# One encoder layer with retrieved experts: projections and attention moved between the expert pairs, three tiles at a time

## The chip, the cores and the metric

One core of a Trainium2 chip runs one launch of the kernel, all in float32. The metric is the device time of that launch in microseconds. Before the change it is 4207.86 us, the median of three runs (4206.48 to 4216.56).

## What is computed

One layer over 1024 prompt tokens and 8 x 16 sample tokens: nine tiles of 128 tokens (eight of the prompt, PT, and one of the samples, ST) by 1024 features.

```python
q_sb, k_sb, v_sb, q_sw, k_sw, v_sw, q_mem, gates = split_projection(rmsnorm(x, norm_mix), w_in, b_gate)
o_sb  = sb_attend(...)    # stick-breaking, 8 heads x 64, over all earlier tokens
o_sw  = sw_attend(...)    # window of 128, 8 heads
o_mem = mem_attend(...)   # 4 heads x 128 into 256 memory tokens
x = x + (sum_b gates_b * (o_b @ w_o_b)) @ w_out
xb = rmsnorm(x, norm_ffn)
# product-key retrieval: 8 heads, the best 16 of 128 x 128 experts each = 128 experts per token
s = einsum('thpd,hpkd->thpk', xb @ w_q, keys);  idx, g = softmax of the best 16 per head
a = gelu(einsum('thkd,td->thk', u_tab[idx], xb))
x = x + einsum('thk,thkd->td', g * a, v_tab[idx])
```

A token's row of expert tables is 2 x 1024 floats (u and v), 8 KB. So a gather of one expert slot for the 128 tokens of a tile is 1 MB, and there are 9 x 128 = 1152 of them, 1208 MB in all. Stick-breaking attention of prompt tile t reads the key blocks t, t-1, ... 0; tiles 0 to 7 make 36 steps of (query tile, key block), the samples two more.

## The kernel before

`build` (L1696) runs three parts, each a block of its own, with every engine's instructions written out by hand and ordered by semaphores.

- `project` (L83): normalises and transposes the nine tiles and two tiles of memory, and makes all of q, k, v. Weight blocks of 2 MB are the outer loop, the tiles the inner one; a unit is eight matmuls into one PSUM bank (L315, and L310 for q of the stick-breaking branch). 61 units.
- `attend` (L527): a software pipeline over steps of time `tau` from the tables of `Course` (L466). A stick-breaking step starts every two `tau` and goes from engine to engine: scores on PE (L815), |z|, exp, ln on ScalarE (L867 to L871), softplus on VectorE (L905), running sums on PE (L682, L685), exp on ScalarE (L829), the carried sum on VectorE (L894), values on PE (L744). Beside it run 27 window and memory units.
- `experts` (L1068): gates, output projections, queries, scores and ranking of a group of tiles (a `Front`, L975, again steps `tau`: the gates' matmuls L1340 and L1350, the output's L1365, the queries' L1388), and the expert pairs. The groups are (0, 1), (2, 3, 4), (5, 6, 7, 8).

The expert part is a sequence of 576 **ticks**, 64 for a tile, each with a **pair** of slots. GpSimd gathers a slot into a ring of RING = 10 buffers (L1311) when PE has released the buffer. VectorE takes the dot product of the u half with the token's row `xp`, which lies in PSUM (L1674, twice a tick). ScalarE makes the gelu (L1497), the weight (L1504, twice) and a diagonal matrix of it (L1510, twice). PE multiplies the v half by the diagonals and adds up in PSUM (L1416, eight matmuls a tick), and so releases the buffers. After its part of the pair each engine does `advance`: the steps `tau` of the next group's Front that `PACES` (L1027) gives this tick. On PE it stands behind the pair's sums. Every second tick VectorE also does a piece of the ranking (`top`, L1531; three pieces for each of a tile's eight heads) of the tiles that are not the first of their group.

```python
            advance(0)
            for m in range(NT):
                for q in range(NB):
                    if q == 0:
                        advance(1 + m * NB)
                    accumulate(m, q)
                    if q:
                        advance(1 + m * NB + q)
```

Of the kernel before, what the change touches and what calls it, by code (L numbers as in the profile page):

```python
# [20 lines left out]
TOK = NT * P  # L31
DB, DS = 8, 16
HD = 64
MH, MD, MT = 4, 128, 256
# [9 lines left out]
RING = 10  # L44
BATCH = 2
NB = SLOTS // BATCH
GROUPS = ((0, 1), (2, 3, 4), (5, 6, 7, 8))
PARTS = (2, 3, 4)
HALF = P // 2
# [29 lines left out]
WQ = 2 * PH * P  # L79
# [3 lines left out]
def project(nc, A, S, small_dram, hT_d):  # L83

    ident = S["const"][:, 0:P]
    hT, mhT, ps = S["hT"], S["mhT"], S["ps"]
    with ExitStack() as ctx:  # L87
        sb = lambda n, s, dt=F32: ctx.enter_context(nc.sbuf_tensor(n, s, dt))
        sem = lambda n: ctx.enter_context(nc.semaphore(n))
        w = S["shared"][:, 0:2 * KC * HB].rearrange("p (a k n) -> p a k n", a=2, k=KC)  # L90
        stage = S["shared"][:, 2 * KC * HB:2 * KC * HB + 4 * HB].rearrange("p (a n) -> p a n", a=4)
        gmix = sb("gmix", [P, 2, KC])
        gq = sb("gq_heads", [P, 2 * HD + 2 * MD])
        ss = sb("ss", [P, 3])
        nrm = sb("nrm", [P, 3, 8])
        XR = 4
        xt = [S["vsb"][:, 2 * i:2 * i + 2, :].rearrange("p a n -> p (a n)") for i in range(XR)]
        sqt = stage[:, 3, :]

        const_in = sem("const_in")  # L100
        gains_in = sem("gains_in")
        gmix_in = sem("gmix_in")
        x_in = [sem(f"x_in{i}") for i in range(XR)]
        w_in = [sem(f"w_in{i}") for i in range(2)]
        x_sq = sem("x_sq")
        x_ms = sem("x_ms")
        x_rt = sem("x_rt")
        x_rs = sem("x_rs")
        x_nat = sem("x_nat")
# [4 lines left out]
        squared = sem("squared")  # L114
        summed = sem("summed")
        mean = sem("mean")
        rooted = sem("rooted")
# [7 lines left out]
        v_out = sem("v_out")  # L125
        cache_out = sem("cache_out")
        spilled = sem("spilled")

        TILES = [A["x_prompt"][0, t * P:(t + 1) * P, :] for t in range(PT)]
        TILES += [A["x_sample"].rearrange("b s d -> (b s) d")]  # L130
        TILES += [A["mem_prompt"][0, t * P:(t + 1) * P, :] for t in range(2)]
        NX = len(TILES)

        w_v = A["w_in"][0].rearrange("(c p) n -> p c n", p=P)
        wm_v = A["w_mem_kv"][0].rearrange("(c p) n -> p c n", p=P)

        BLOCKS = [("ksb", w_v[:, :, 512:1024], 512, range(NT)), ("vsb", w_v[:, :, 1024:1536], 512, range(NT)),
                  ("kvsw", w_v[:, :, 2048:2304], 256, range(NT)), ("qsw", w_v[:, :, 1536:2048], 512, range(NT)),
                  ("qm", w_v[:, :, 2304:2816], 512, range(NT)), ("mk", wm_v[:, :, 0:512], 512, range(2)),
                  ("mv", wm_v[:, :, 512:1024], 512, range(2)), ("qsb", w_v[:, :, 0:512], 512, range(12))]  # L140
        units = [(c, kind, t) for c, (kind, _, _, tiles) in enumerate(BLOCKS) for t in tiles]

        n_copy, n_norm, n_turn = [], [], []
        a = b = d = 0
        slots, s = [], 0
        n_out = [0, 0, 0]
        outs_before = []
        for _, kind, t in units:
            a += kind in ("ksb", "vsb", "mv", "qsb", "kvsw")
            b += kind in ("kvsw", "qsw", "qm", "mk")  # L150
            turns = kind in ("ksb", "kvsw", "qsw", "qm", "mk")
            d += turns
            n_copy.append(a)
            n_norm.append(b)
            n_turn.append(d)
            slots.append(s % 3 if turns else None)
            outs_before.append(n_out[s % 3] if turns else 0)
            if turns:
                if kind in ("ksb", "mk"):
                    n_out[s % 3] += 1  # L160
                if kind == "kvsw" and t == PT - 1:
                    n_out[s % 3] += 1
                if kind == "kvsw" and t == ST:
                    n_out[s % 3] += DB
                s += 1
        FINAL_OUT = list(n_out)
        last_of = {c: max(u for u, x in enumerate(units) if x[0] == c) for c in range(len(BLOCKS))}
        copies = ("ksb", "vsb", "mv", "qsb", "kvsw")
        norms = ("kvsw", "qsw", "qm", "mk")
# [5 lines left out]
        def bank(u):  # L175
            return u % NPB

        def turn_bank(n):
            return 3 if n < NT else 3 + n % 2
# [1601 lines left out]
```

## Time and profile before

| | |
|---|---|
| median of three runs | 4207.86 us |
| the profiled execution: its own time | 4207.44 us |
| the profiled execution: its span | 4205.6 us |
| PE busy | 3254.9 us (77%) |
| VectorE busy | 2448.8 us (58%) |
| ScalarE busy | 1249.4 us (30%) |
| GpSimd busy | 1098.0 us (26%) |
| moved by DMA | 1399 MB, 1208 MB of it gathers |

### The profile page before, as it was taken

To read this page: it belongs to the slowest core of one execution; us is meant where nothing else is said; L and a number is where in the kernel's file an instruction comes from. 1 tells how busy PE (TensorE), PEld (TensorE's weight loads), DVE (VectorE), ACT (ScalarE), POOL (GpSimd) and SP (SyncE) were. 2 spreads that over 40 slices of the span, in tenths; PEclk is the share of its full clock that TensorE was granted. 3 is DMA by queue.
4 is the path that set the end of the run, shared out by engine and by line. 5 is a ranking of instruction groups with operands and counts; after the bars stand their busy time and mean duration, and the time that the engine had idled before them with its cause. 6 is when DMAs were issued, how large, how long until landed. Compare 5 with 4: busy or idle time off the path is not lost.

```text
span 4205.6 us, 46334 instructions
## 1 busy us (share of the span) xinstructions
PE 3254.9 (77%) x16665; PEld 1443.1 (34%) x16665; DVE 2448.8 (58%) x5586; ACT 1249.4 (30%) x3959; POOL 1098.0 (26%) x1167
## 2 busy tenths in 40 slices
PE   8999999898779998778888887985555555555555
PEld 4545665587424454322222242431111111111111
DVE  2131456512957756857757765785775775776444
ACT  2111467601422223322222224332222222222222
POOL 0000000000333323333333333333333333333332
PEclk9999899999889999989999998987777777777777
DMA  4301320044999999999999999999999999999998
GB/s 139 113 20 66 122 76 16 21 163 158 419 420 420 415 414 417 393 421 421 420 417 421 419 414 421 421 396 417 421 418 417 417 411 413 419 413 417 421 421 342
DMA packets 242087, 1399.44 MB, mean 333 GB/s; under 512 B 26544, under 2 KB 54448, under 8 KB 89008
## 3 DMA queue, kind: packets, MB, share of 16 engines
q0 software_dynamic: 165888, 1208.03, 69.6%
q1 hardware_dynamic: 75968, 188.44, 12.1%
q8 instruction: 131, 2.15, 0.2%
q14 instruction: 100, 0.82, 0.0%
HBM read 1366.49 MB, written 30.80 MB: 332 GB/s over the span
## 4 chain that ended last, share of the span: by engine, by line
DMA 38%; PE 22%; DVE 14%; issue 3%; ACT 2%; POOL 1%; another core or an unknown queue 0%; DVEq 0%; ACTq 0%; POOLq 0%
DMA ring<-in_experts_dram,idx 38%; PE ps L1416 10%; DVE ring L1674 6%; PE ps L1340 4%; PE ps L1388 4%; PE ps L1365 2%; PE ps L1350 2%; ACT diag L1510 1%; DVE hot L1564 1%; DVE hot L1560 1%; DVE idx L1568 1%; POOL ring L1311 1%; ACT wgt L1504 1%; DVE flat L1556 1%; DVE flat L1553 1%
## 5 line engine op out<-in xcount | busy, mean ns | idle before, releaser
L1416 PE MATMUL ps<-ring,diag 64*64 64x512 f32 x9216 | 1445.0, 757 | 870.1 <-ACT diag L1510 856.9
L1674 DVE CUSTOM_DVE_ANT_0 ring<-ring,ps 128x1024 f32<-128x1024 f32 x1152 | 1390.3, 1220 | 962.8 <-DMA ring<-in_experts_dram,idx 902.0
L1311 POOL DMA_INDIRECT ring<-in_experts_dram,idx x1152 | 1092.0, 948 | 2665.5 <-PE ps L1416 1900.8
L1416 PEld LDWEIGHTS ps<-ring,diag 64*64 64x64 f32 x9216 | 356.1, 159 | 1868.8 <-ACT diag L1510 1298.3
L1497 ACT ACTIVATE act_<-hid 128x2 f32<-128x2 f32 x576 | 117.2, 204 | 2075.8 <-DVE hid L1674 2008.9
L1340 PE MATMUL ps<-shared 128*128 128x256 f32 (+2 forms) x1152 | 409.3, 502 | 5.5 <-PEq L535 4.5
L1510 ACT ACTIVATE diag<-const,wgt 128x64 f32<-128x64 f32 x1152 | 337.9, 340 | 18.8
L1340 PEld LDWEIGHTS ps<-shared 128*128 128x128 f32 x1152 | 215.1, 194 | 207.3 <-issue 151.0
L315 PE MATMUL ps<-shared,hT 128*128 128x512 f32 (+1 forms) x720 | 284.8, 551 | 1.8 <-DVE mhT L429 1.3
L1504 ACT ACTIVATE wgt<-act_,gw 128x1 f32<-128x1 f32 x1152 | 276.7, 287 | 20.6 <-ACT act_ L1497 0.4
L1388 PE MATMUL ps<-shared 128*128 128x256 f32 (+2 forms) x768 | 273.6, 505 | 1.2 <-ACT shared L1459 1.2
L1350 PE MATMUL ps<-o_x,shared 128*128 128x256 f32 (+2 forms) x576 | 207.4, 497 | 0.0
L1388 PEld LDWEIGHTS ps<-shared 128*128 128x128 f32 x768 | 143.8, 195 | 143.9 <-issue 110.2
L315 PEld LDWEIGHTS ps<-shared,hT 128*128 128x128 f32 x720 | 134.3, 191 | 131.2 <-issue 124.9
L905 DVE SCALAR_TENSOR_TENSOR sps<-ps,za 128x512 f32<-128x512 f32 x76 | 52.3, 688 | 201.0 <-ACT za L871 201.0
L1350 PEld LDWEIGHTS ps<-o_x,shared 128*128 128x128 f32 x576 | 106.1, 191 | 100.3 <-issue 75.6
L1365 PE MATMUL ps<-shared,mixn 128*128 128x256 f32 x576 | 132.5, 386 | 1.6 <-DVE mixn L1614 1.6
L1365 PEld LDWEIGHTS ps<-shared,mixn 128*128 128x128 f32 x576 | 108.5, 192 | 38.4 <-issue 24.4
L440 DVE TENSOR_REDUCE nrm<-shared 128x4 f32<-128x512 f32 (+2 forms) x29 | 16.3, 561 | 179.7 <-ACT shared L366 179.7
L682 PE MATMUL ps<-sps,const 128*128 128x512 f32 x152 | 95.7, 714 | 30.9 <-DVE sps L911 17.0
L667 POOL MEMSET shared<- 128x4096 f32 x1 | 3.5, 3515 | 412.1 <-POOLq L87 412.1
L1674 DVE DVE_READ_ACCUMULATOR2_ANT hid<- 128x1 f32 x1152 | 94.6, 82 | 0.0
(178 smaller groups left out, 2512.4 us busy)
## 6 DMA issues: line engine op xcount, KB each, us to landing
shared<-in_w_gate_o_dram SPq DMA_DIRECT2D x72, 768.0 KB
shared<-in_w_q_dram SPq DMA_DIRECT2D x24, 1024.0 KB
ring<-in_experts_dram,idx POOLq DMA_INDIRECT x1152
shared<-in_w_out_dram SPq DMA_DIRECT2D x12, 1024.0 KB
shared<-in_w_in_dram SPq DMA_DIRECT2D x5, 2048.0 KB, 8.1
o_x<-o_scratch SPq DMA_DIRECT2D x9, 768.0 KB
hT_scratch<-hT SPq DMA_DIRECT2D x9, 512.0 KB, 6.5
shared<-hT_scratch SPq DMA_DIRECT2D x9, 512.0 KB
```

The source lines that it names most:

```text
L315: last = nc.tensor.matmul(ps[:, bank(u), 0:n], src[:, k, t * P:(t + 1) * P], w[:, c % 2, k, 0:n], start=(k == 0), stop=(k == KC - 1))
L682: last = nc.tensor.matmul(z, tri, sps[:, x % 3], start=False, stop=True, skip_group_check=True)
L1311: i = nc.gpsimd.indirect_dma_start(out=ring[:, j % RING, :], out_offset=None, in_=A["experts"], in_offset=bass.IndirectOffsetOnAxis(ap=idx ...
L1340: last = nc.tensor.matmul(ps[:, 4 + u % 2, 0:N].rearrange("p (i t) -> p i t", t=P), w[:, k * P:(k + 1) * P], hx[:, 0:n, k, :], start=(k == ...
L1350: last = nc.tensor.matmul(ps[:, 6 + u % 2, 0:N].rearrange("p (i t) -> p i t", t=P), w[:, k * P:(k + 1) * P], o[:, 0:n, b, k - KC, :], star ...
L1365: last = nc.tensor.matmul(ps[:, 4 + x % 4, 0:2 * P], mixn[:, k * N + i * P:k * N + (i + 1) * P], w[:, k * 2 * P:(k + 1) * 2 * P], start=(k ...
L1388: last = nc.tensor.matmul(ps[:, 4 + x % 2, 0:N].rearrange("p (i t) -> p i t", t=P), w[:, c:c + P], hx[:, 0:n, k, :], start=(k == 0), stop= ...
L1416: last = nc.tensor.matmul(acc[ROWS[r ^ h], h, :], diag[ROWS[r], j % 4, :], ring[ROWS[r], j % RING, DM + h * HB:DM + (h + 1) * HB], start=( ...
L1497: nc.scalar.activation(act_[:, c], hid[:, c], ACT.Gelu_apprx_tanh).then_inc(gelus, 1)
L1504: last = nc.scalar.activation(wgt[:, i:i + 1], act_[:, i:i + 1], ACT.Copy, scale=gw[:, m % 2, i:i + 1])
L1510: last = nc.scalar.activation(diag[:, j % 4, :], ident2, ACT.Copy, scale=wgt[:, j % SLOTS:j % SLOTS + 1])
L1674: last = nc.vector.tensor_tensor_reduce(out=u, in0=u, in1=xp, scale=1.0, scalar=0.0, op0=ALU.mult, op1=ALU.add, accum_out=hid[:, j % SLOTS ...
```

## The change

The whole kernel becomes one function, `layer`, with one block.

- The nine tiles run in the order 0, 1, ST, 2, ..., 7, in three groups of N = 3. For each group a **chain** of steps `tau` is made: `project` (its three tiles; the first group has the memory too), `attend`, `front`. A chain has 240, 245 and 279 steps; 48 and 48 of those of the second and third group are projections, 57 and 91 attention, 140 and 140 the front.
- Of the first chain 209 steps run ahead of all ticks (`advance(0)`), up to the first ranked head. Its last 31 lie in ticks 0 to 25, the second chain in ticks 26 to 183, the third in ticks 192 to 375 (1.55 and 1.52 steps a tick); ticks 376 to 575 carry none.
- The projections' weights are loaded once per group, 11 MB for each of the later two. `hT`, the queries and the attention's results stay in SBUF instead of going through DRAM.
- In `attend` a stick-breaking step starts every four `tau` (`PACE`), with one buffer `za` instead of two and two score banks instead of four; window units start every 3, 6 or 8.
- The ring has 7 buffers. `xp` is in SBUF.
- On PE `advance` stands ahead of `accumulate` in every tick, on ScalarE and VectorE behind the pair's part as before.
- In the 160 ticks that carry projections or attention (26 to 93 and 192 to 283, `EXP_FORM`), gelu is made from exp and ln: VectorE forms the polynomial in four small operations, ScalarE does exp, ln, exp in place of one gelu. The reciprocal roots are made from ln and exp too, with three small VectorE operations (`refine`).

The diff is a rewrite of the file; its core:

```diff
-RING = 10
+RING = 7
-GROUPS = ((0, 1), (2, 3, 4), (5, 6, 7, 8))
-PARTS = (2, 3, 4)
+N = 3
+COLS = N * P
+NGROUPS = NT // N
+ORDER = (0, 1, ST, 2, 3, 4, 5, 6, 7)
+TILES_OF = tuple(ORDER[N * g:N * g + N] for g in range(NGROUPS))
+PARTS = 3
...
+LENGTH = [J.length[g] + C.length[g] + FRONTS[g].steps for g in range(NGROUPS)]
...
-    done = FRONTS[0].first_head
+    done = J.length[0] + C.length[0] + FRONTS[0].first_head
...
+def exp_form():
+
+    at, spans = 0, []
+    for g in range(NGROUPS):
+        spans.append((at, at + J.length[g] + C.length[g]))
+        at += LENGTH[g]
+    out, done = [], PACES[0]
+    for T in range(NT * NB):
+        to = done + PACES[1 + T]
+        out.append(any(done <= b and to > a for a, b in spans[1:]))
+        done = to
+    return out
...
-        xp = ps[:, 2:4, :].rearrange("p a n -> p (a n)")
+        xp = sb("xp", [P, DM])
...
-            chain = (0 for f in FRONTS for _ in front(f))
+            chain = (0 for g in range(NGROUPS) for stage_of in (project, attend, front) for _ in stage_of(g))
...
@@ tensor
             for m in range(NT):
-                for q in range(NB):
-                    if q == 0:
-                        advance(1 + m * NB)
-                    accumulate(m, q)
-                    if q:
-                        advance(1 + m * NB + q)
+                for tick in range(NB):
+                    advance(1 + m * NB + tick)
+                    accumulate(m, tick)
@@ scalar, of one tick
+                    if EXP_FORM[T]:
+                        n_exp += 1
+                        nc.scalar.activation(act_[:, c], act_[:, c], ACT.Exp, scale=-GELU_B).then_inc(gelus, 1)
+                        act.wait_ge(gelus, T + 1)
+                        nc.scalar.activation(act_[:, c], act_[:, c], ACT.Ln, bias=1.0).then_inc(logged, 1)
+                        act.wait_ge(logged, n_exp)
+                        nc.scalar.activation(act_[:, c], act_[:, c], ACT.Exp, scale=-1.0).then_inc(sigmas, 1)
@@ vector, of one tick
+                    if EXP_FORM[T]:
+                        link(last)
+                        c = recent(tick)
+                        link(nc.vector.scalar_tensor_tensor(out=cube[:, 0, :], in0=hid[:, c], scalar=GELU_A, in1=hid[:, c], op0=ALU.mult, op1=ALU.mult))
+                        nc.vector.tensor_tensor(gx[:, c], hid[:, c], gw[:, m % 2, tick * BATCH:(tick + 1) * BATCH], ALU.mult)
+                        link(nc.vector.scalar_tensor_tensor(out=cube[:, 1, :], in0=cube[:, 0, :], scalar=1.0, in1=hid[:, c], op0=ALU.add, op1=ALU.mult))
+                        last = nc.vector.tensor_scalar(act_[:, c], cube[:, 1, :], -GELU_FAR, None, ALU.max)
                     last.then_inc(dots, 1)
```

How that stands on the engines. PE in the front of the second group, before: the pair's sums are L1416, the gates' matmuls L1340 and L1350.

```order
L1416 MATMUL ps<-ring,diag 64x512 x8
L1340 MATMUL ps<-shared 128x384 x8
L1416 MATMUL ps<-ring,diag 64x512 x8
L1350 MATMUL ps<-o_x,shared 128x384 x4
L1416 MATMUL ps<-ring,diag 64x512 x8
L1340 MATMUL ps<-shared 128x384 x8
```

PE in the attention of the second group, after the change: the pair's sums are L1177, the running sums L951 and L954, scores L1084, values L1014, windows L970, L1026 and L1043.

```order
L1177 MATMUL ps<-ring,diag 64x512 x8
L1026 MATMUL ps<-const,over 128x128 x4
L951 MATMUL ps<-over,const 128x512
L954 MATMUL ps<-over,const 128x512
L970 MATMUL ps<-kswT,oq 128x256 x4
L1014 MATMUL ps<-over,vsb 64x128 x8
L1043 MATMUL ps<-over,vsw 64x128 x8
L1177 MATMUL ps<-ring,diag 64x512 x8
L951 MATMUL ps<-over,const 128x512
L954 MATMUL ps<-over,const 128x512
L1177 MATMUL ps<-ring,diag 64x512 x8
```

The work of attention, which stood in a part of its own with no pairs, now stands in short pieces between the pairs' sums; each piece waits for ScalarE and VectorE.

VectorE in two ticks there, after the change: the dots are L1740, the polynomial L1745 to L1748, the carried sum L1520, softplus L1531.

```order
L1740 ISA ring,hid<-ring,xp 128x1024 [waits ring_in4,link_]
L1740 ISA hid 128x1
L1740 ISA ring,hid<-ring,xp 128x1024 [waits ring_in5]
L1740 ISA hid 128x1
L1745 SCALAR_TENSOR_TENSOR cube<-hid 128x2 [waits link_]
L1746 TENSOR_TENSOR gx<-hid,gw 128x2 [waits link_]
L1747 SCALAR_TENSOR_TENSOR cube<-cube,hid 128x2
L1748 TENSOR_SCALAR act_<-cube 128x2 [waits link_]
L1520 TENSOR_TENSOR over<-over 128x512 [waits latered,sums]
L1531 SCALAR_TENSOR_TENSOR over<-ps,over 128x512 [waits latered,sums,logd]
L1740 ISA ring,hid<-ring,xp 128x1024 [waits sp_raw,ring_in6]
```

The softplus of this tick (it waits for `logd`, ScalarE's ln) stands ahead of the next tick's dots on the same engine.

## Rows read from the trace of the kernel before

**Rows 1.** The page: busy tenths in 40 slices of the span.

```profile
PE   8999999898779998778888887985555555555555
...
DMA  4301320044999999999999999999999999999998
```

**Rows 2.** Busy time by stretch: start:end, us, then PE, PEld, DVE, ACT, POOL, clock, DMA, GB/s.

```profile
0.00:413.00 413.00, 395.39 (x1189) 209.34 (x1189) 83.68 (x189) 71.85 (x172) 0.55 (x6) 0.99 0.24 82
413.00:850.00 437.00, 388.18 (x2828) 258.18 (x2828) 239.32 (x406) 262.46 (x594) 5.45 (x9) 0.90 0.19 62
850.00:1052.80 202.80, 187.96 (x864) 163.97 (x864) 36.98 (x109) 24.97 (x48) 6.56 (x7) 0.97 0.47 166
...
1203.40:1826.60 623.20, 556.88 (x2776) 260.36 (x2776) 415.49 (x1015) 179.51 (x602) 195.93 (x204) 0.93 1.01 413
...
3179.50:4205.00 1025.50, 573.85 (x3216) 136.57 (x3216) 632.43 (x1358) 268.34 (x1016) 371.43 (x393) 0.74 0.99 409
```

**Rows 3.** The same by stretch for the dots, L1674, alone; four records a tick.

```profile
1052.80:1203.40 150.60, 62.46 (x104) 0.79 1.01 420
1203.40:1826.60 623.20, 246.49 (x408) 0.93 1.01 413
1826.60:2179.20 352.60, 155.38 (x256) 0.95 1.01 419
2179.20:3179.50 1000.30, 446.29 (x736) 0.86 1.01 417
3179.50:4205.00 1025.50, 487.44 (x800) 0.74 0.99 409
```

**Rows 4.** Groups by line and form: busy us, mean ns of one, idle before.

```profile
L1674 DVE CUSTOM_DVE_ANT_0 ring<-ring,ps 128x1024 f32<-128x1024 f32 x1152 | 1390.3, 1220 | 962.8 <-DMA ring<-in_experts_dram,idx 902.0 <-issue 48.5 <-DVE gw L1581 2.5
L315 PE MATMUL ps<-shared,hT 128*128 128x512 f32 x576 | 253.1, 594 | 1.8 <-DVE mhT L429 1.3 <-DVE vsb L417 0.4
L1340 PE MATMUL ps<-shared 128*128 128x384 f32 x384 | 131.2, 495 | 0.0
L1365 PE MATMUL ps<-shared,mixn 128*128 128x256 f32 x576 | 132.5, 386 | 1.6 <-DVE mixn L1614 1.6
L905 DVE SCALAR_TENSOR_TENSOR sps<-ps,za 128x512 f32<-128x512 f32 x76 | 52.3, 688 | 201.0 <-ACT za L871 201.0
L871 ACT ACTIVATE za<-za 128x512 f32<-128x512 f32 x76 | 47.9, 630 | 2.4
L1558 DVE TENSOR_SCALAR part<-flat 128x16 uint32<-128x16 uint32 x72 | 13.1, 182 | 2.5
```

**Rows 5.** Timeline of PE in two ticks of the front of group (2, 3, 4).

```profile
1339.56 1.95 PE L1416 MATMUL ps<-ring,diag 64*64 64x512 f32 x16
...
1341.44 5.43 PE L1340 MATMUL ps<-shared 128*128 128x384 f32 x16
...
1351.45 1.95 PE L1416 MATMUL ps<-ring,diag 64*64 64x512 f32 x16
```

**Rows 6.** Timeline of one pair in the last stretch, from dot to release.

```profile
3513.54 1.22 DVE L1674 CUSTOM_DVE_ANT_0 ring<-ring,ps 128x1024 f32<-128x1024 f32 x1 [0.80 <-DMA ring<-in_experts_dram,idx]
...
3517.30 0.20 ACT L1497 ACTIVATE act_<-hid 128x2 f32<-128x2 f32 x1 [3.79 <-DVE hid L1674]
...
3518.68 3.40 PE L1416 MATMUL ps<-ring,diag 64*64 64x512 f32 x16 [2.63 <-ACT diag L1510]
...
3520.97 0.94 POOL L1311 DMA_INDIRECT ring<-in_experts_dram,idx  x1 [3.70 <-PE ps L1416]
```

**Rows 7.** Timeline: the first gather of all and its dot.

```profile
1044.41 1.11 POOL L1311 DMA_INDIRECT ring<-in_experts_dram,idx  x1 [625.75 <-DVEq L1584]
...
1052.82 1.22 DVE L1674 CUSTOM_DVE_ANT_0 ring<-ring,ps 128x1024 f32<-128x1024 f32 x1 [7.38 <-DMA ring<-in_experts_dram,idx]
```

**Rows 8.** Timeline: a gather that starts inside an operation with two SBUF inputs.

```profile
1578.05 1.29 DVE L1634 SCALAR_TENSOR_TENSOR mixn<-o_x,p_nrm,gffn 128x1024 f32<-128x1024 f32 x1
1578.41 1.74 POOL L1311 DMA_INDIRECT ring<-in_experts_dram,idx  x1 [0.30 <-issue]
```

More of the change, by code:

```diff
@@ L30 @@
 NT = PT + 1
-TOK = NT * P
 DB, DS = 8, 16
 HD = 64
+HALF = P // 2
 MH, MD, MT = 4, 128, 256
@@ new lines, with paces @@
+J = Proj()
+C = Course()
+FRONTS = [Front(g) for g in range(NGROUPS)]
+FIRST_OF = {f.base: f for f in FRONTS}
+RANK_LEAD = 26
+LENGTH = [J.length[g] + C.length[g] + FRONTS[g].steps for g in range(NGROUPS)]
+def paces():
+    total = [sum(LENGTH[:g + 1]) for g in range(NGROUPS)]
+    done = J.length[0] + C.length[0] + FRONTS[0].first_head
+    out = [done]
+    ticks = N * NB
+    for g in range(NGROUPS):
+        goal = total[g + 1] if g + 1 < NGROUPS else done
+        lead = 0 if g else RANK_LEAD
+        start, mid = done, total[0] if lead else done
+        for i in range(ticks):
+            if i < lead:
+                to = start + -(-(mid - start) * (i + 1) // lead)
+            else:
+                to = min(goal, mid + -(-(goal - mid) * (i + 1 - lead) // (ticks - 8 - lead))) if g + 1 < NGROUPS else done
+            out.append(to - done)
+            done = to
+    return out
@@ new lines @@
+PACES = paces()
+def exp_form():
+    at, spans = 0, []
+    for g in range(NGROUPS):
+        spans.append((at, at + J.length[g] + C.length[g]))
[4 more added lines that the diff above has]
+        out.append(any(done <= b and to > a for a, b in spans[1:]))
+        done = to
+    return out
+EXP_FORM = exp_form()
+TOP_AT = {m: (m - 1) * NB + (30 if m == 1 else 18 if m == 2 else 6) for m in range(1, NT) if m not in FIRST_OF}
@@ new lines, in layer @@
+        vsw = sb("vsw", [P, PT + 1, P])
+        mkT = sb("mkT", [P, MH, MT])
+        mv = sb("mv", [P, 2, MH * MD])
+        hx = sb("hx", [P, N, KC, P])
+        oq = sb("oq", [P, 5 * DM])
+        over = sb("over", [P, 9 * DM])
+        stage_ = sb("stage", [P, 4 * HB])
+        ring = sb("ring", [P, RING, 2 * DM])
+        xrow = sb("xrow", [P, DM])
+        xp = sb("xp", [P, DM])
+        side = sb("side", [P, DM])
+        s = sb("s", [P, 2 * PH * NK])
+        diag = sb("diag", [P, 4, HALF])
@@ L137, in project @@
[L137 to L169, printed above, removed]
-        heads = {"kvsw": (KVH, HD), "qsw": (SWH, HD), "qm": (MH, MD), "mk": (MH, MD)}
-        gain_of = {"qsw": gq[:, 0:HD], "kvsw": gq[:, HD:2 * HD], "qm": gq[:, 2 * HD:2 * HD + MD],
-                   "mk": gq[:, 2 * HD + MD:2 * HD + 2 * MD]}
-        NPB = 3
-        def bank(u):
-            return u % NPB
@@ L1322, in _, with turn @@
         def _(pe):
-            def front(f):
-                g, n, N = f.g, f.n, f.cols
+            def turn(u):
+                n = J.n_turn[u] - 1
+                if n >= 1:
+                    pe.wait_ge(kept, n)
+                if J.units[u][1] == "ksb":
+                    pe.wait_ge(copied, J.n_copy[u])
+                else:
+                    pe.wait_ge(gained, J.n_norm[u])
+                m = 1 if J.units[u][1] == "kvsw" else 4
+                for j in range(m):
+                    last = nc.tensor.transpose(ps[:, 5, j * P:(j + 1) * P], stage[:, J.slot[u], j * P:(j + 1) * P], ident)
+                last.then_inc(turned, 1)
```

2202 lines of the change are left out of this document (1109 added, 1093 removed).

## The prediction

> **What bounds the kernel now.** The first view is the page's strip of 40 slices [rows 1]. It has two halves: for ten slices PE is at 8 or 9 tenths and DMA at 0 to 4; from the eleventh on DMA is full, with PE at 7 to 9 tenths and then, for the last third, at 5. The second view cuts the span at the stages [rows 2]: projections 413 us, attention 437 us, the first front 203 us until the first dot at 1052.8, all at PE, with DMA moving 62 to 166 GB/s; then the experts, DMA share 1.01, 413 to 420 GB/s. So 1053 us pass before a gather's data are used. The change starts the gathers earlier, with a third of the work done, and carries the rest between the pairs.
>
> The third view counts ticks [rows 3]; four records are a tick. Ticks 0 to 25 take 150.6 us (5.8 each). Ticks 26 to 127, with the front of three tiles, take 623.2 (6.1). The last 200 ticks carry none and take 1025.5 less the tail: 5.1 each, which is 2.1 MB at 413 GB/s. All 576 average 5.47. The question is what a tick costs that carries projections or attention.
>
> **The start.** The first group's projections are 23 units. A wide one is 7.0 us (253.1 us for 36, [rows 4]); 16 wide, 3 half and 4 of 384 columns (8 matmuls of 0.68, 5.4) make 145, with transposes, first loads and drain 186. Its attention has 5 of 38 steps and 9 of 27 window units, and all of the sample caches' work. Of the 437 us [rows 2] the steps' share is 57 and the window units' 146; they overlap, the caches add, and a step now starts only every fourth `tau`: I take 155 (bounds 130 and 180). The front has 384 columns where it had 256: 288 gate matmuls at 0.68 [rows 4, 5] are 196, 96 of the output at 0.46 [rows 4] 44, norm, first head and first gather 51, so 291 where it was 203 [rows 2]. First dot at 632 us, bounds 580 and 690: **421 us gained**. Ticks 0 to 25 stay at 151 [rows 3].
>
> **A tick with attention.** VectorE comes first. Two dots back to back are 2.4 us [rows 4]. The polynomial is four operations of the smallest kind (0.18 each, [rows 4]) with gaps, 0.8. Ranking is 145 us for 16 heads (632.4 busy less 487.4 of dots, [rows 2, 3]), 9.1 a head or 1.5 a tick while it runs. The second group's attention brings 12 steps and 9 window units: 24 softplus at 0.69 [rows 4], 18 carried sums and 18 masks of the same size, and three passes of the dots' size per window, 83 us in 37 ticks; the third's is 108 us in 60. So VectorE is busy 6.9 and 6.1 us a tick, over the 5.1 of DMA by itself.
>
> Then the waits, which no row shows, since attention and pairs never met. A softplus waits for three ScalarE operations of 0.6 each [rows 4], 1.9. Where two `tau` fall into one tick (half of the ticks), and one is the softplus' own, ScalarE comes to them only behind its part of the pair: 1.4 us from the last dot to PE's start [rows 6] and 0.5 for two more small operations. So the softplus stands 3.9 us after the dots, VectorE has had 1.4 us of other work at most, and the next tick's dots are queued behind. That is 2.6 us in a quarter of the ticks, 0.7 a tick; window units (a norm that waits for five exponentials), masks and the seams add 0.9. I take 8.5 and 7.6 us. Bounds: nothing (6.9 and 6.1), and each hop in series, 11.
>
> **A tick with projections.** PE's work is 126 us for a group of three (12 wide units 84, 3 half and 4 of 384 columns 32, transposes 10) in 31 ticks, with pairs' sums of 1.95 [rows 5] and 0.3 for the switch: 6.3. VectorE's norms wait on ScalarE in the same way. I take 7.4 in 31 ticks and 7.3 in 32; bounds 6.3 and 9.
>
> **A tick with a front.** Two ticks now take 11.89 us, with PE without a gap [rows 5]. At 1.55 instead of 1.5 steps a tick that is 6.2. PE's new order (chain, then sums) takes nothing from PE; it fills the wait for the diagonals, and it delays a release by a piece of chain, up to 5.4 us.
>
> That meets **the ring of 7**. In the steady stretch a buffer is held 7.4 us from its dot to its next gather [rows 6]; a lone gather needs 8.4 us to its dot [rows 7]. Seven buffers at 2.5 us are 17.5 us, so 1.7 us are spare where ten left 9. A gather that starts in an operation with two SBUF inputs runs 1.74 instead of 0.94 us [rows 8], and the dots have two such inputs now. A piece of ranking (5.7 us at most) holds a pair 3 us longer. I add 0.1 to each of the last 200 ticks (bounds 0 and 0.5) and 0.2 to each tick with a front (0 and 0.6). The page "DMA: Bandwidth & Descriptors" of the Trainium skill (section on the anatomy of one DMA by SWDGE) fits one such DMA as about 2.0 us plus its bytes at 436 GB/s, 4.4 us for a gather. The rows show 8.4 from issue to dot, so I don't use it; by it the ring would cost nothing and the sum be 56 us lower.
>
> **The sum**: 632 + 151 + 31 x 7.4 (229) + 37 x 8.5 (315) + 90 x 6.4 (576) + 8 ticks between (45) + 32 x 7.3 (234) + 60 x 7.6 (456) + 92 x 6.4 (589) + 200 x 5.2 (1040) + 9 of tail = 4276 of span, and with the 2 us between span and own time **4278 us**. That profiled execution, 4207.44, is the median of the runs (4207.86), so no correction. The extra reads (11 MB of weights for each of two groups, 55 us at 420 GB/s) cost nothing by themselves: they fall in ticks of over 7 us, where DMA has 2 us to spare. If these ticks came down to 5.5 they would be the bound.
>
> **The rivals.**
> (a) The waits are covered, faster. VectorE may run up to three pairs ahead, and PE's early chain step makes most results ready. With all waits at zero the sum is 4028 (attention 621 us, projections 6.8 a tick, fronts 6.15, the last ticks 5.1); with half of them, about 4150. For it: the front's ticks lose little to such waits today, PE being busy 89% of that stretch [rows 2]. Against: there nobody waits inside a tick; softplus does. It decides once a third of the 250 us of waits in my sum falls away. Chance 0.35.
> (b) Each tick of attention pays its hops in series, 11 us: 97 x 3 = 290 more, 4570. For it: attention alone takes 11.5 us a step [rows 2] with engines that do nothing else. Chance 0.11.
> (c) The ring of 7 starves the gathers, since bursts are the rule: 0.4 us more in 382 ticks, 4430. Chance 0.10.
> (d) The start is not cut as the schedule says: attention of the first group and its caches take 80 us more, 4360. Chance 0.05.
> (e) The dots wait for the gathers. By the page "SBUF — State Buffer" of the Trainium skill (section on the two separate sides) the port pair that VectorE and GpSimd share is an exclusive lock, and whichever starts second "fully blocks". Rows 8 show one side of it: the gather waited, and the operation took its 1.29 us. Were the dots to wait too, up to 0.94 each, ticks with attention or projections would take about 0.5 us more: 80 us, 4360. Chance 0.04.
> The forecast itself, 4195 to 4345, has 0.35, of it 0.06 within 0.3% (13 us, about what a measurement of this kernel can tell from none). Faster by more 0.35, within 0.3% 0.06, slower by more 0.59. The range leaves out the ends of (a) and (b): 4040 to 4540.
>
> **What would show it.** The first dot near 632 us. In ticks 57 to 93 and 224 to 283 DMA under full (270 to 300 GB/s), VectorE over 80% busy, its idle time before the softplus ended by ScalarE's ln; PE's granted clock below the 0.93 of today's front. In the last 200 ticks 5.2 us a tick, VectorE's idle time ended by gathers, GpSimd's gathers longer than 0.94 us. Wrong would be: DMA full in the ticks with attention (then (a)), a first dot after 700 us (d), or over 5.5 us a tick at the end (c).

## The result, and the profile after

| | before | after |
|---|---|---|
| median of the undisturbed runs | 4207.86 us (3 runs) | 4568.99 us (3 runs) |
| ratio of their times | | 1.085, 95% interval 1.0824 to 1.0874 |
| span of the profiled execution | 4205.6 | 4567.2 |
| first dot | 1052.8 | 656.6 |
| table loads on ScalarE | 63 | 600 |

Slower by 8.5%, where 1.7% was forecast; 4569 lies above the range's end of 4540. One of four runs of each kernel, disturbed (6306 and 9722 us), is left out. The loads are counted over the whole trace.

The page of the kernel after, busy tenths in 40 slices; the rows of PE and DMA answer to [rows 1].

```profile
PE   8988987766666999886775565699988555555555
...
ACT  4531024656887322325567788832232222222222
...
DMA  5222359766655999998865556699999999999999
```

DMA is now under full twice after the gathers have begun, in slices 8 to 13 and 19 to 26 (counted from one). There ScalarE is at 5 to 8 tenths, and 8 is the most it has anywhere.

The kernel after by stretch: start:end, us, then PE, PEld, DVE, ACT, POOL, clock, DMA, GB/s, in the form of [rows 2]. They are projections and attention of the second group, its front, the same three of the third group, and the last 200 ticks.

```profile
811.00:1101.00 290.00, 212.47 (x863) 88.53 (x855) 155.70 (x482) 181.55 (x364) 65.72 (x61) 0.84 0.69 264
1101.00:1483.00 382.00, 230.62 (x1360) 101.49 (x1356) 235.17 (x618) 297.98 (x571) 76.24 (x76) 0.76 0.59 212
1483.00:2050.00 567.00, 521.25 (x2578) 251.20 (x2576) 370.00 (x899) 161.68 (x543) 197.18 (x180) 0.96 1.00 404
...
2093.00:2385.00 292.00, 212.76 (x863) 87.46 (x855) 157.91 (x480) 185.06 (x368) 62.38 (x61) 0.85 0.73 272
2385.00:2974.00 589.00, 343.95 (x2100) 144.05 (x2100) 340.10 (x898) 487.67 (x896) 124.24 (x123) 0.78 0.61 223
2974.00:3543.00 569.00, 520.16 (x2609) 251.65 (x2608) 363.43 (x858) 162.35 (x551) 204.56 (x184) 0.97 1.00 405
3543.00:4567.00 1024.00, 559.29 (x3216) 134.28 (x3216) 632.50 (x1355) 266.32 (x1016) 433.76 (x396) 0.76 1.00 413
```

Cut at each tick's first dot, and set beside the forecast and the first experiment, `e1_tables` (all in us a tick, but the first row; the last row runs to the end of the span, tail included, which the forecast's 5.2 leaves out; without the tail the measured ones are 5.08):

| ticks | carry | before | forecast | after | e1_tables |
|---|---|---|---|---|---|
| first dot | | 1052.8 | 632 | 656.6 | 643.8 |
| 0-25 | rest of first front | 5.79 | 5.8 | 5.92 | 5.97 |
| 26-56 | projections | 5.96 | 7.4 | 9.37 | 7.28 |
| 57-93 | attention | 6.16 | 8.5 | 10.32 | 8.15 |
| 94-183 | front | 5.76 | 6.4 | 6.30 | 6.26 |
| 192-223 | projections | 5.56 | 7.3 | 9.14 | 7.15 |
| 224-283 | attention | 5.74 | 7.6 | 9.81 | 7.44 |
| 284-375 | front | 5.20 | 6.4 | 6.18 | 6.20 |
| 376-575 | nothing | 5.13 | 5.2 | 5.12 | 5.13 |

The loss stands in the 160 ticks with projections or attention. They took 1553 us, where the same ticks took 935 before and 1234 were forecast; every other stretch is within 25 us of its forecast. What the forecast did not have in them is in the groups of ScalarE, kernel after: line, operation, count, busy us, mean ns, idle before.

```profile
L1394 ACT ACT_TABLE_LOAD x160 | 205.3, 1283 | 2.8
L1396 ACT ACT_TABLE_LOAD x160 | 205.3, 1283 | 2.9
...
L1316 ACT ACT_TABLE_LOAD x76 | 97.5, 1283 | 1.4
...
L1392 ACT ACT_TABLE_LOAD x44 | 56.5, 1283 | 0.8
...
L1256 ACT ACT_TABLE_LOAD x29 | 37.2, 1283 | 0.5
L1258 ACT ACT_TABLE_LOAD x29 | 37.2, 1283 | 0.5
```

Lines 1392 to 1396 are the pair's exponential form (exponential, logarithm, exponential), 1316 is the chain's logarithm, 1256 and 1258 are logarithm and exponential of a norm. In these lines a load of 1.28 us stands ahead of each change from exponential to logarithm or back. The kernel before names one table set with both functions, `natural_log_exp_and_others`, at the head of its attention (its line 821); the changed kernel has no such line. Ahead of the first dot it has 56 loads where 7 stood before, and in the 160 ticks 499 where 22 stood. The timeline shows them in place; kernel after, one tick of attention.

```profile
2604.65 0.20 ACT L1396 ACTIVATE act_<-act_ 128x2 f32<-128x2 f32 x1
2604.66 0.17 DVE L1748 TENSOR_SCALAR act_<-cube 128x2 f32<-128x2 f32 x1
...
2606.04 3.69 PE L1177 MATMUL ps<-ring,diag 64*64 64x512 f32 x16 [6.07 <-ACT diag L1414]
...
2606.50 0.63 ACT L1314 ACTIVATE over<-over 128x512 f32<-128x512 f32 x1
...
2607.15 1.28 ACT L1316 ACT_TABLE_LOAD   x1
...
2608.44 0.63 ACT L1316 ACTIVATE over<-over 128x512 f32<-128x512 f32 x1
2609.09 1.28 ACT L1392 ACT_TABLE_LOAD   x1
2609.10 0.69 DVE L1531 SCALAR_TENSOR_TENSOR over<-ps,over 128x512 f32<-128x512 f32 x1 [3.95 <-ACT over L1316]
...
2610.38 0.20 ACT L1392 ACTIVATE act_<-act_ 128x2 f32<-128x2 f32 x1
...
2610.61 1.28 ACT L1394 ACT_TABLE_LOAD   x1
...
2611.90 0.20 ACT L1394 ACTIVATE act_<-act_ 128x2 f32<-128x2 f32 x1
...
2612.12 1.28 ACT L1396 ACT_TABLE_LOAD   x1
```

VectorE finished the input of the next pair at 2604.83; ScalarE, still at the pair before, comes to it at 2609.09. PE waited 6.07 us for diagonals, VectorE 3.95 us for the chain's logarithm, and its next dots were behind that. These hand-overs by themselves could still be the price, as rival (b) had it: its 4570 is the measured time. Only an experiment separates the two.

### The profile page after: what moved, and what is told of

It reads as the page before. It is cut to its first block, busy times and chain, and to the rows that moved or that the text cites. A ratio compares the mean times of both kernels' runs of the same rounds, so it can differ in the third digit from the quotient of the medians.

```text
span 4567.2 us, 47872 instructions
## 1 busy us (share of the span) xinstructions
PE 3318.5 (73%) x16665; PEld 1485.3 (33%) x16665; DVE 2543.6 (56%) x6300; ACT 1999.6 (44%) x4853; POOL 1249.0 (27%) x1167
## 4 chain that ended last, share of the span: by engine, by line
PE 39%; DMA 20%; ACT 18%; DVE 18%; issue 5%; POOL 1%; SPq 0%; DVEq 0%; ACTq 0%; POOLq 0%
DMA ring<-in_experts_dram,idx 20%; PE ps L1177 11%; DVE ring L1740 7%; PE ps L1106 7%; PE ps L911 4%; PE ps L1149 4%; PE ps L1111 4%; PE ps L1126 3%; ACT L1396 3%; ACT L1394 3%; ACT diag L1414 2%; ACT L1316 1%; ACT wgt L1408 1%; PE ps L1084 1%; PE ps L906 1%
## 5 line engine op out<-in xcount | busy, mean ns | idle before, releaser
L1177 PE MATMUL ps<-ring,diag 64*64 64x512 f32 x9216 | 1429.6, 748 | 1001.1 <-ACT diag L1414 984.2
L862 POOL DMA_INDIRECT ring<-in_experts_dram,idx x1152 | 1243.6, 1079 | 3141.5 <-PE ps L1177 2511.7
L1740 DVE CUSTOM_DVE_ANT_0 ring<-ring,xp 128x1024 f32<-128x1024 f32 x1152 | 1389.4, 1224 | 828.0 <-DMA ring<-in_experts_dram,idx 807.8
L1177 PEld LDWEIGHTS ps<-ring,diag 64*64 64x64 f32 x9216 | 351.8, 158 | 1906.4 <-ACT diag L1414 1344.9
L1106 PE MATMUL ps<-hx,over 128*128 128x384 f32 x1152 | 400.1, 496 | 7.3 <-DMA over<-in_w_gate_o_dram 7.3
L911 PE MATMUL ps<-over,hx 128*128 128x512 f32 (+1 forms) x720 | 314.5, 590 | 0.0
L1106 PEld LDWEIGHTS ps<-hx,over 128*128 128x128 f32 x1152 | 214.4, 191 | 202.4 <-issue 70.8
L1149 PE MATMUL ps<-hx,over 128*128 128x384 f32 x768 | 264.6, 494 | 1.2 <-ACT hx L1352 1.2
L1531 DVE SCALAR_TENSOR_TENSOR over<-ps,over 128x512 f32<-128x512 f32 x76 | 52.6, 692 | 300.7 <-ACT over L1316 292.1
L1396 ACT ACT_TABLE_LOAD x160 | 205.3, 1283 | 2.9
L1394 ACT ACT_TABLE_LOAD x160 | 205.3, 1283 | 2.8
L1111 PE MATMUL ps<-oq,over 128*128 128x384 f32 x576 | 199.8, 490 | 0.0
L911 PEld LDWEIGHTS ps<-over,hx 128*128 128x128 f32 x720 | 142.7, 205 | 152.5 <-issue 147.6
L1149 PEld LDWEIGHTS ps<-hx,over 128*128 128x128 f32 x768 | 140.5, 190 | 134.1 <-issue 49.8
L951 PE MATMUL ps<-over,const 128*128 128x512 f32 x152 | 110.3, 815 | 69.0 <-DVEq L1539 40.0
L1111 PEld LDWEIGHTS ps<-oq,over 128*128 128x128 f32 x576 | 107.6, 190 | 88.4 <-issue 17.1
L1126 PE MATMUL ps<-over 128*128 128x256 f32 x576 | 129.3, 383 | 1.9 <-DVE over L1678 1.9
```

The source lines that it names most:

```text
L862: i = nc.gpsimd.indirect_dma_start(out=ring[:, j % RING, :], out_offset=None, in_=A["experts"], in_offset=bass.IndirectOffsetOnAxis(ap=idx ...
L911: last = nc.tensor.matmul(ps[:, J.bank(u), 0:n], src, w[:, b % 2, k, 0:n], start=(k == 0), stop=(k == KC - 1))
L1106: last = nc.tensor.matmul(ps[:, 4 + u % 2, 0:COLS].rearrange("p (i t) -> p i t", t=P), wb[:, k * P:(k + 1) * P], hx[:, :, k, :], start=(k ...
L1111: last = nc.tensor.matmul(ps[:, 6 + u % 2, 0:COLS].rearrange("p (i t) -> p i t", t=P), wb[:, k * P:(k + 1) * P], q[:, :, b, k - KC, :], st ...
L1126: last = nc.tensor.matmul(ps[:, 4 + x % 4, 0:2 * P], mixn[:, k * COLS + i * P:k * COLS + (i + 1) * P], wb[:, k * 2 * P:(k + 1) * 2 * P], s ...
L1149: last = nc.tensor.matmul(ps[:, 4 + x % 2, 0:COLS].rearrange("p (i t) -> p i t", t=P), wb[:, c:c + P], hx[:, :, k, :], start=(k == 0), sto ...
```

## The experiments

Times and ratios below are against runs of the kernel before on the same chip (4206 to 4212 us). "Set kept" means that the edit stands on the first experiment's kernel.

**1. The set named once.**

```diff
+            nc.scalar.preload_act_table_set("natural_log_exp_and_others")
             advance(0)
...
                     if EXP_FORM[T]:
                         n_exp += 1
+                        if not EXP_FORM[T - 1]:
+                            nc.scalar.preload_act_table_set("natural_log_exp_and_others")
```

> The changed kernel with one thing added: the table set that holds both exponential and logarithm is loaded on ScalarE before the first chain and again at the first pair of each stretch with the exponential form (ticks 26 and 192), and stays. Theory A (the 498 table loads of 1.28 us in the four stretches with the exponential form set their ticks, in series between dots and sums and between the chain's exponential and VectorE's softplus): the loads of those stretches go from 498 to a handful, attention ticks fall from 10.3 and 9.8 us to about 7.0, projection ticks from 9.4 and 9.1 to about 7.2, the time from 4569 to 4080-4200 us. Theory B (the loads lie beside other work, and the hand-overs between engines are the price, as in the prediction's rival of series hops): attention ticks stay above 9 us, the time above 4430 us. The stretches 94-191 and 284-575 do not move in either (6.3, 6.2 and 5.1 us a tick).

4204.4 us, ratio 0.9986 (0.9977 to 0.9996). The loads fell from 600 to 49, the time by 365 us. Theory A stands for the cause, a little outside its numbers (4204 for at most 4200, attention 8.15 and 7.44 where about 7.0 was expected). 551 loads less are 707 us of ScalarE and 365 of time, 0.66 us for one of 1.28; in the 160 ticks it is 351 us (1553 to 1202) for 497 loads, 0.71 each. Theory B falls: attention ticks without loads are 8.15 and 7.44 us. The attention of the second and of the third group in the first experiment, windows as above:

```profile
1025.00:1326.00 301.00, 204.24 (x1331) 92.41 (x1324) 233.69 (x616) 142.29 (x445) 78.93 (x74) 0.83 0.73 269
...
2162.00:2608.00 446.00, 313.58 (x2080) 136.10 (x2076) 338.81 (x898) 225.80 (x690) 131.09 (x121) 0.86 0.78 292
```

In the third group ScalarE went from 488 to 226 us, the stretch from 589 to 446. The waits there (us in total, times, longest) before the edit, in the changed kernel (the first experiment's are shown under the second):

```profile
POOL ring L862 <- PE ps L1177: 449.6, 87, 15.9
...
PE ps L1177 <- ACT diag L1414: 205.8, 38, 10.8
DVE over L1531 <- ACT over L1316: 143.1, 31, 10.1
```

VectorE's wait for the logarithm went from 143 to 58 us, PE's for the diagonals from 206 to 95.

**2. PE's order undone, set kept.**

```diff
                 for tick in range(NB):
-                    advance(1 + m * NB + tick)
                     accumulate(m, tick)
+                    advance(1 + m * NB + tick)
```

> The first experiment's kernel (table set kept) with PE's order undone: the pair's weighted sums ahead of the chain's step of the tick, in all ticks. Theory A (PE has room in every stretch, so its order only shifts waits of a microsecond): within 30 us of the first experiment, either side; buffers come free earlier and softplus or its sums come later. Theory C (sums behind the step hold the ring back in attention ticks, where POOL waited longest for PE): the attention and projection ticks fall by 0.5 us or more, 80 us or more in all. Theory D (the order is needed: with sums first the chain's step of PE waits for ScalarE's diagonals each tick): attention ticks grow by over 0.5 us, 50 us or more in all.

4514.9 us, ratio 1.0723 (1.0705 to 1.0741): 310 us over the first experiment, theory D. Attention ticks go from 8.15 and 7.44 to 11.22 and 10.46 us, projections by 0.3, fronts and the rest not at all. The waits in the third group's attention, first experiment:

```profile
POOL ring L862 <- PE ps L1177: 298.1, 76, 12.1
...
PE ps L1177 <- ACT diag L1417: 94.6, 27, 7.8
DVE over L1534 <- ACT over L1316: 58.0, 19, 5.9
...
ACT over L1274 <- PE ps L954: 21.8, 13, 4.1
```

and with the sums first:

```profile
POOL ring L862 <- PE ps L1177: 498.5, 99, 17.3
...
PE ps L1177 <- ACT diag L1417: 264.4, 54, 13.6
ACT over L1274 <- PE ps L954: 153.3, 35, 6.7
...
DVE over L1523 <- PE ps L954: 87.4, 20, 8.8
```

PE stands at the diagonals with the chain's step behind it. ScalarE then waits for that step's sums, with the next pair queued behind its wait, and VectorE waits for them too. The loop closes over three engines. The release that frees buffers does not come earlier either: POOL waits 200 us more.

**11. The same with the loads left in** (the changed kernel, PE's order alone undone).

> The changed kernel as it is (with its 600 table loads) and PE's order undone: the pair's weighted sums ahead of the chain's step of the tick. Theory A (by the second experiment, attention ticks grow by 3 us and projection ticks by 0.3 where PE must wait for the diagonals before it scores for the chain; loads on the same path add to it): 4569 plus 280 to 450 us, 4850-5020. Rival (loads already set the tick and hide the order): within 60 us of 4569.

5011.3 us, ratio 1.1914 (1.1894 to 1.1934), 442 over the changed kernel. The loads cost 365 us with the chain first and 496 with the sums first (5011 less 4515), so loads and order together cost 132 us more than the two prices added up. Theory A, 4850 to 5020, stands.

**3 and 4. The ring of 7, and the token's row in SBUF,** each in the kernel before; 4 has both.

```diff
-RING = 10
+RING = 7
...
-        xp = ps[:, 2:4, :].rearrange("p a n -> p (a n)")
+        xp = sb("xp", [P, DM])[:, :]
```

> The kernel before with the ring of expert rows cut from 10 to 7 buffers and nothing else. Theory A: no difference over 0.3% (4195-4220 us), since a pair's rows are asked for over two ticks (10 us) ahead and land in under 9. Rival (the ring starves when something holds the sums back): 20 us or more slower, in the ticks with the next stage's work.

> The kernel before with the ring of 7 (as in the third experiment) and the token's row in SBUF in place of PSUM, so that the dots read two SBUF operands. Theory A: dots stay at 1.22 us, gathers' time on POOL grows from 0.95 to about 1.1 us as in the changed kernel, and the time is within 0.3% of the third experiment. Rival (the dots wait for the gathers' descriptors or these for the dots long enough to be late): gathers near 1.9 us or dots above 1.3 us, and 30 us or more over the third experiment.

Ring: 4227.2 us, ratio 1.0045 (1.0028 to 1.0061), small but there: 19 us, where theory A had none and the rival 20 or more. It stands in ticks 57-93 (6.32 for 6.16 us) and 94-183 (5.83 for 5.76); the last 200 stay at 5.13. Row in SBUF on top: 4230.6 us, 1.0049 (1.0032 to 1.0066), no difference: theory A. The gathers' groups of the third and the fourth experiment, and the dots' of the fourth:

```profile
L1311 POOL DMA_INDIRECT ring<-in_experts_dram,idx x1152 | 1089.7, 946 | 2693.2 <-PE ps L1416 1939.9
```

```profile
L1311 POOL DMA_INDIRECT ring<-in_experts_dram,idx x1152 | 1266.5, 1099 | 2524.0 <-PE ps L1416 1760.9
L1674 DVE CUSTOM_DVE_ANT_0 ring<-ring,xp 128x1024 f32<-128x1024 f32 x1152 | 1398.1, 1226 | 978.6 <-DMA ring<-in_experts_dram,idx 967.5
```

A gather on POOL took 0.15 us more, the dots 6 ns. What the ring of 7 costs in the changed kernel's own ticks with attention no run shows, since none of that kernel has ten buffers.

**5. Ranking ahead of the chain's step on VectorE** in the 160 ticks, set kept. The block with `SHIFTED`, `RANKED` and `WEIGHED` is unchanged.

```diff
-                    advance(1 + T)
+                    if not EXP_FORM[T]:
+                        advance(1 + T)
                     if T in SHIFTED:
...
                         weigh(*WEIGHED[T])
+                    if EXP_FORM[T]:
+                        advance(1 + T)
```

> The first experiment's kernel (table set kept, 4204 us) with one thing moved on VectorE: in the 160 ticks with the exponential form the ranking of the next tiles (maximum, shift, weights) stands between the dots and the chain's step instead of behind it. Theory A (in those ticks VectorE waits for ScalarE's logarithm of the same tick, 87 us in the attention stretches, while ranking work that waits for nothing stands behind that wait): the ranking covers part of it, and the time falls by 20 to 60 us, to 4145-4185. Rival (the chain's step, now 1 to 3 us later, makes PE's step and the sums behind it late): 0 to 60 us slower than the first experiment.

4163.6 us, ratio 0.9882 (0.9866 to 0.9899), 41 us better than the first: theory A. Attention ticks 7.70 and 6.99 us; the wait for the logarithm in the third group's attention went from 58.0 to 41.7 us, PE's for diagonals from 94.6 to 60.7.

**6. ScalarE's step ahead of its part of the pair, and 7. both.**

```diff
                     c = recent(tick)
+                    if EXP_FORM[T]:
+                        advance(1 + T)
                     act.wait_ge(dots, T + 1)
...
-                    advance(1 + T)
+                    if not EXP_FORM[T]:
+                        advance(1 + T)
```

> The first experiment's kernel with one thing moved on ScalarE: in the 160 ticks with the exponential form the chain's step stands ahead of the pair's part (three small activations, weights, diagonals) instead of behind it. Theory A (the series dots, pair's part, chain's exponential and logarithm, softplus, next dots sets attention ticks; ahead of the pair the logarithm is ready when the dots end): VectorE's idle time ahead of softplus goes from 87 us to near nothing and the time falls by 40 to 120 us, to 4085-4165. Rival (ScalarE's step waits for PE or VectorE work of the same tick, so the pair's diagonals and with them the sums and gathers are late): POOL's and PE's waits grow, and the time is 40 us or more over the first experiment.

> The fifth and sixth experiments together. Theory A: the gains overlap, since both remove the same wait: no more than 20 us better than the better of the two. Rival: with ScalarE's step ahead of the pair and VectorE's step behind its ranking, ScalarE waits for VectorE's results of the step while the pair's part stands behind that wait: 50 us or more slower than the sixth.

4262.6 us (ratio 1.0115, 1.0098 to 1.0132) and 4279.0 us (1.0153, 1.0136 to 1.017): the theory falls, the rival holds, but by stage. Attention ticks grow to 8.92 and 8.58 us, while projection ticks fall from 7.28 and 7.15 to 6.77 and 6.68. In attention the sixth shows why; waits as above:

```profile
PE ps L1177 <- ACT diag L1419: 171.2, 51, 7.4
ACT over L1274 <- PE ps L954: 146.0, 34, 6.8
DVE over L1537 <- ACT over L1316: 57.9, 16, 8.8
```

ScalarE waited 146 us for PE's sums over keys (21.8 in the first experiment) with the diagonals behind that wait, and VectorE's wait did not shrink at all (57.9 for 58.0). The seventh was expected 50 us or more over the sixth by its rival; it is 16. Its theory A, that two gains overlap, doesn't fit either: the sixth was no gain, and the two together are 115 us over the fifth alone.

**8. Gelu from its own table in all ticks,** the shared set loaded before the chain's step: two loads a tick where the changed kernel has three.

```diff
-EXP_FORM = exp_form()
+STAGE_TICK = exp_form()
+EXP_FORM = [False] * len(STAGE_TICK)
...
+                    if STAGE_TICK[T]:
+                        nc.scalar.preload_act_table_set("natural_log_exp_and_others")
                     advance(1 + T)
```

> The changed kernel without its exponential form: Gelu from its own table in all ticks, and in the 160 ticks that carry projections or attention the set with exponential and logarithm loaded before the chain's step, so two loads a tick, 320 in all (410 us of ScalarE) in place of 498. Theory A (a load in these ticks cost 0.53 to 0.59 us of the time, by the changed kernel against the first experiment; the exponential form saves loads but costs about 0.7 us a tick of small operations on the path): 320 loads cost some 180 us over the first experiment, less 110 for the small operations: 4250-4300 us. Rival (the small operations of the exponential form are the larger price): under 4204 us. Rival (a load between dots and sums costs its whole 1.28 us): 4400 us or more.

4211.8 us, ratio 1.0001 (0.9991 to 1.001). 317 loads in those ticks came to the same as the exponential form with 2, within 0.15%. None of the three expectations was right. The nearest is the rival of small operations that cost more than the loads (under 4204). Theory A had 4250 to 4300; its price of a load was too low (0.53 to 0.59 us is the share of its time, per load it is 0.71), and if 0.71 holds here too, the form's own price, 0.7 us a tick in theory A, is 1.4. Attention ticks are 8.11 and 7.47 us, 8.15 and 7.44 with the exponential form. VectorE was busy 305 us instead of 339 in the third group's attention, ScalarE 361 instead of 226:

```profile
2164.00:2612.00 448.00, 314.50 (x2078) 137.75 (x2078) 304.99 (x657) 360.62 (x687) 131.97 (x121) 0.86 0.78 290
```

So what the form saves in loads, two a tick, it costs again by its own operations on both engines; which of them costs how much was not taken apart.

**12. Loads where DMA is full,** set kept; two loads between dots and Gelu in 190 ticks.

```diff
                     else:
+                        if 94 <= T < 184 or 376 <= T < 476:
+                            nc.scalar.preload_act_table_set("natural_log_exp_and_others")
                         nc.scalar.activation(act_[:, c], hid[:, c], ACT.Gelu_apprx_tanh).then_inc(gelus, 1)
```

> The first experiment's kernel with two table loads (2.56 us) put between dots and Gelu in 190 ticks that carry no chain with logarithms: 94 to 183 (the fused projections ahead of the experts, with DMA full) and 376 to 475 (nothing but the pairs, DMA full). Theory A (a load costs time where the loop over engines sets the tick, none where DMA does, as long as the ring covers it): 94-183 within 0.2 us of 6.26 us a tick, 376-475 within 0.1 of 5.13, total within 20 us of 4204. Rival (a load between dots and sums always delays the gather that follows it): 376-475 at 6 us or more and 94-183 above 7 us a tick, 150 us or more in all.

4261.7 us, ratio 1.0127 (1.011 to 1.0144), 57 over the first. Theory A is nearer, and too low: 94-183 went from 6.26 to 6.64 us a tick, 35 us for 173 loads more; 376-575 grew by 30.5 us for 198, nearly all of it in 376-475 (5.13 to 5.42 a tick). A load there costs 0.15 to 0.20 us, against 0.71 in the 160 ticks. In these ticks, where DMA is full, most of a load is hidden, not all.

**9 and 10. A version faster than both.** The ninth is the fifth with the sixth's order in the 63 ticks with projections alone (`PROJ_TICK`). The tenth also puts VectorE's step of an attention tick without ranking behind the next tick's first dot:

```diff
                     for j in range(m * SLOTS + tick * BATCH, m * SLOTS + (tick + 1) * BATCH):
+                        if j % BATCH == 1 and T and LATE_TICK[T - 1]:
+                            advance(T)
                         dve.wait_ge(ring_in[j % RING], 16 * (j // RING + 1))
```

> The fifth experiment's kernel (table set kept, ranking ahead of the chain's step on VectorE) with ScalarE's step ahead of the pair's part in the 63 ticks with projections alone. Theory A (the sixth experiment's order helped where ScalarE's step only copies and squares what PE has finished, 6.77 and 6.68 against 7.28 and 7.15 us a tick, and hurt in attention, where the exponential of the sums waits for PE): projection ticks at 6.7 us, the rest as in the fifth, 4135-4155 us. Rival (the gains are the same wait, already covered by the ranking moved ahead): within 0.3% of the fifth (4151-4176).

> The ninth experiment's kernel with VectorE's step of an attention tick without ranking put behind the first dot of the next tick. Theory A (VectorE's wait for the logarithm is covered by a dot that waits for nothing, 1.3 us a tick in about 50 of the 97 attention ticks): attention ticks fall by 0.2 to 0.6 us, 20 to 55 us in all. Rival (softplus later makes PE's sums over keys, and with them ScalarE's exponential of the weights, late by as much; the loop runs through PE and ScalarE too): no gain, or up to 60 us slower than the ninth.

4138.0 us, ratio 0.9832 (0.9814 to 0.985), and 4125.2 us, 0.9808 (0.9791 to 0.9824). The ninth is inside its theory A (4135 to 4155). The tenth gained 13 us, where its theory A had 20 to 55 and its rival none: attention ticks fell by 0.12 and 0.16 (7.75 and 6.93 in the ninth). Against the kernel before the tenth is 1.9% faster. Its ticks: projections 6.70 and 6.65 us, attention 7.63 and 6.77, fronts 6.37 and 6.19, the rest 5.13.

## Why the prediction was wrong

The direction was right and the size was not. **The step that failed** is in "A tick with attention": the softplus was put 3.9 us behind the dots, by "1.4 us from the last dot to PE's start and 0.5 for two more small operations". The two operations are 0.2 us each, as said; the two table loads between them, 2.6 us, were not counted, nor the one ahead of the chain's logarithm or the two in a norm. The line that names the set stood in the attention of before and doesn't stand in the kernel after; the change was read for what it added and not for what it dropped. The same fault is in the terms for projections and for the start. With the loads gone, and nothing else changed, every term of the sum comes out within 5%:

- **The sum.** Forecast 4276 of span, first experiment 4204. The 72 us between them are projections 4 + 5, attention 13 + 10, fronts 13 + 19 and the last ticks with the tail 23, all taken somewhat high, less 12 for the start and 3 for the rest, taken low.
- **The start**: 632 forecast, 656.6 measured, 643.8 without loads. 51 loads there, 65 us of ScalarE, cost 13.
- **A tick with attention**: 8.5 and 7.6 forecast, 10.32 and 9.81 measured, 8.15 and 7.44 without loads. VectorE was to be over 80% busy; it was 62% and 58%, and 78% and 76% in the first experiment (234 of 301 us, 339 of 446). Its idle time before the softplus was ended by ScalarE's logarithm, as said (143 us in the third group, 58 in the first experiment). That the first experiment lands so near is in part luck: VectorE's work there is 6.3 and 5.6 us a tick where 6.9 and 6.1 were put, and its idle time 1.8 where 1.6 and 1.5 were. The 83 us of attention work in the step are too many by its own terms too, which add to about 75 (24 and 36 operations of 0.69, 27 of 1.22). DMA was to move 270 to 300 GB/s; it moved 212 and 223, and 269 and 292 without loads. The granted clock, said to be under 0.93, was 0.76 and 0.78, and 0.83 and 0.86 without loads.
- **A tick with projections**: 7.4 and 7.3 forecast, 9.37 and 9.14 measured, 7.28 and 7.15 without loads.
- **A tick with a front**: 6.4 forecast, 6.30 and 6.18 measured. The step went by PE's work alone. DMA's share is 1.00 there (404 GB/s), and PE is busy 5.8 us of the tick (521 of 567 us), so both are near their limit; which of them sets the tick was not taken apart.
- **The ring of 7**: 0.1 added to each of the last 200 ticks and 0.2 to each with a front. In the last 200 it cost nothing (5.12), and in the kernel before it costs 0.45% of the whole (third experiment), in earlier ticks. The estimate by the page "DMA: Bandwidth & Descriptors" of the Trainium skill, by which the ring would cost nothing, gives the right answer for the last 200 ticks only.
- **PE's new order** "takes nothing from PE" and fills the wait: right, but not where the prediction said it. The step speaks of ticks with a front, and there the order is worth nothing (6.26 and 6.27, 6.20 and 6.16 us); its 310 us with the set kept, 442 without, are nearly all in attention. The prediction gave it no number.
- **Rival (b)**, hops in series at 11 us a tick, gives 4570 and would have been read as confirmed by the total alone. Its mechanism is refuted by the first experiment. Rival (c) did not come (5.12 in the last ticks, fronts under their forecast), (d) was 25 us at the start and 12 without loads instead of 80, and (e) is refuted: the dots took 1.224 us against 1.220 [rows 4], while gathers went from 0.948 to 1.079.
- **Rival (a)**, waits covered at 4028 to 4150, needed two repairs: the set named, and the order of VectorE and ScalarE mended (tenth experiment, 4125, inside the rival's range).

A page of the Trainium skill bears on the step that failed. The traces first: 1283 ns a load, and the next operation starts 10 to 20 ns behind it (2610.61 + 1.28, then 2611.90). "ScalarE: Activation LUTs" of the Trainium skill (section on what ACT_TABLE_LOAD costs) has the same 1283 ns and adds 1.38 us for a drain, which no row here shows. Its section on table sets counts one load for logarithm then exponential, since one set holds both; here that held only where the kernel named the set, and without it a load stood ahead of each of the two. "ScalarE activation tables: per-element evaluation and per-set limits" of the Trainium skill (section on the compiler and the runtime) says that the compiler places loads by longest run within a block. Taken by its words that does not describe these rows: exponential, logarithm and exponential follow each other in a tick, one set holds both, and still 160 loads stand ahead of the second and 160 ahead of the third.

## What to carry to other kernels

When work is taken from one phase into another, list what the old phase set up for itself as well as its operations: a table set, a mode, a buffer. Count table loads by line in the first trace after any change on ScalarE; one of 1.28 us cost 0.7 us of time in ticks whose loop runs over four engines, and 0.15 to 0.20 where DMA was full. In such a loop the order on an engine can be worth as much as its work (PE's order 310 us here, the loads 365). Decide it stage by stage: ScalarE's order of the sixth experiment gained 31 us in projections and lost 97 in attention.

## What the runs showed of the hardware

- The contention between a VectorE operation with two SBUF inputs and a gather on POOL went one way. With the token's row in SBUF the gathers rose from 0.946 to 1.099 us and the dots from 1.220 to 1.226. Sorted by their starts in the fourth experiment's trace, the 414 gathers that began inside a dot took 1.36 us and the other 738 took 0.95 (0.94 and 0.95 in the third); the 508 dots that began inside a gather took 1.226, like the rest. "SBUF — State Buffer" of the Trainium skill (section on the two separate sides) has whichever starts second wait; only the gathers did.
- The granted clock followed the waits: 0.76 and 0.78 in the two attention stretches with loads, 0.83 and 0.86 without. The pair's sums behind 6.07 us of idle time took 3.69 us in the timeline above, at a granted clock of 0.50 (the first row below, kernel after), and 1.95 where PE had been busy [rows 5], at 1.00 (the second, kernel before; both in the form of [rows 2]). These are the clock's two levels, 1.2 and 2.4 GHz. So such a wait ahead of PE is paid a second time in the matmuls behind it.

```profile
2606.00:2609.80 3.80, 3.76 (x17) 0.94 (x17) 0.69 (x1) 3.72 (x5) 0.94 (x1) 0.50 0.23 95
```

```profile
1339.50:1341.50 2.00, 2.00 (x18) 0.58 (x17) 1.10 (x3) 0.58 (x1) 0.55 (x1) 1.00 1.00 418
```

- Ten buffers against seven were worth 0.45% in the kernel before (third experiment), though the steady last third showed nothing of it.
